# One layer block's gate projection and attention output as seven products with accumulating transfers

## The reference

```python
def gated_rmsnorm(y, z, w):
    g = (y * jax.nn.silu(z)).astype(jnp.float32).reshape(b, l, N_SSM_GROUPS, D_INNER // N_SSM_GROUPS)
    g = g * lax.rsqrt(jnp.mean(g * g, axis=-1, keepdims=True) + RMS_EPS)
    return (g.reshape(b, l, D_INNER) * w.astype(jnp.float32)).astype(y.dtype)

def hybrid_layer(x, w_in, conv_w, conv_b, dt_bias, a_log, d_skip, ssm_norm_w, sinks, w_out, ln_g, ln_b):
    proj = jnp.einsum("bld,de->ble", x, w_in)
    q, k, v, z_attn, z_ssm, xbc, dt_raw = jnp.split(proj, IN_SPLITS, axis=-1)
    attn = sliding_window_attention(q, k, v, sinks) * jax.nn.silu(z_attn)
    xbc = jax.nn.silu(causal_depthwise_conv(xbc, conv_w, conv_b))
    ...
    y = ssd_chunked(xs, dt, a, bm, cm)
    y = y + (xs.reshape(b, l, N_SSM_HEADS, SSM_HEAD_DIM) * d_skip[:, None]).reshape(b, l, D_INNER)
    ssm = gated_rmsnorm(y, z_ssm, ssm_norm_w)
    out = jnp.einsum("ble,ed->bld", jnp.concatenate([attn, ssm], axis=-1), w_out)
    return layer_norm(DEEPNORM_ALPHA * x + out, ln_g, ln_b)
```

## Time and profile before

| | |
|---|---|
| median of 3 runs | 1929.64 us |
| the profiled execution | 1927.62 us |
| its span | 1925.8 us |
| PE busy in the span | 1566.3 us (81%) |
| DVE, ACT busy | 681.8 us (35%), 304.8 us (16%) |
| PE clock in the first 500 us | full (1.00) |

### The profile page before, as it was taken

One profiled execution on the slowest core, in us unless ns is written; L12 is line 12 of the kernel. 1 busy time (PEld: TensorE's weight loads), 2 busy tenths in 40 slices (PEclk: granted clock), 3 DMA queues, 4 the chain that ended last, 5 costly groups with the idle time before them and its releaser, 6 DMA issues.

```text
span 1925.8 us, 20585 instructions
## 1 busy us (share of the span) xinstructions
PE 1566.3 (81%) x8874; PEld 892.2 (46%) x8874; DVE 681.8 (35%) x1395; ACT 304.8 (16%) x804; POOL 13.0 (1%) x39
## 2 busy tenths in 40 slices
PE   9999999999999999766555656655665556799999
PEld 7775567755667845222212222212222122357886
DVE  3663455634486864311111111101111111144533
ACT  1343313432122102000000000000000000213220
POOL 0000000000000000000000000000000000000000
PEclk9999999999999999978778888788887888899999
DMA  9851376414243456999999999999999999954300
GB/s 378 280 151 46 107 275 219 131 53 165 97 171 136 176 218 264 429 430 430 432 431 428 433 428 430 434 428 431 429 429 432 432 431 428 375 197 171 127 10 22
DMA packets 87779, 554.35 MB, mean 288 GB/s; under 512 B 4512, under 2 KB 11424, under 8 KB 74112
## 3 DMA queue, kind: packets, MB, share of 16 engines
q1 hardware_dynamic: 86544, 548.81, 71.0%
q0 software_dynamic: 1136, 4.10, 0.6%
HBM read 551.85 MB, written 1.05 MB: 287 GB/s over the span
## 4 chain that ended last, share of the span: by engine, by line
PE 60%; DMA 35%; DVE 4%; ACT 1%; issue 0%; POOL 0%; SPq 0%; DVEq 0%; ACTq 0%; POOLq 0%
PE bank L679 27%; DMA ring<-in_w 22%; DMA arena<-in_w 12%; PE bank L1174 8%; PE bank L706 7%; PE bank L688 6%; PE bank L1202 3%; PE bank L667 3%; PE bank L1487 1%; PE bank L878 1%; PE bank L811 1%; PE bank L791 1%; DVE arena L2427 0%; PE bank L1145 0%; PE bank L1225 0%
## 5 line engine op out<-in xcount | busy, mean ns | idle before, releaser
L1174 PE MATMUL bank<-ring,arena 128*32 128x512 f32 x1216 | 283.4, 726 | 147.1 <-DMA arena<-in_w 96.7
L1174 PE MATMUL bank<-arena 128*32 128x512 f32 x832 | 228.9, 722 | 101.1 <-DMA ring<-in_w 101.1
L679 PE MATMUL bank<-ring,arena 128*128 128x512 f32 (+3 forms) x744 | 304.5, 560 | 0.8 <-ACT tmp L1543 0.8
L679 PE MATMUL bank<-arena,ring 128*128 128x256 f32 (+1 forms) x1632 | 291.9, 337 | 0.5 <-DVE arena L3106 0.5
L679 PEld LDWEIGHTS bank<-arena,ring 128*128 128x128 f32 x1632 | 256.5, 191 | 30.6 <-issue 7.5
L679 PEld LDWEIGHTS bank<-ring,arena 128*128 128x128 f32 x744 | 138.5, 191 | 129.9 <-issue 118.6
L1174 PEld LDWEIGHTS bank<-ring,arena 128*32 128x32 f32 x1216 | 71.4, 131 | 266.6 <-issue 266.6
L1202 PE MATMUL bank<-ring,arena 128*32 128x512 f32 x576 | 126.4, 681 | 27.8 <-DMA arena<-in_w 18.8
L1174 PEld LDWEIGHTS bank<-arena 128*32 128x32 f32 x832 | 56.3, 130 | 186.2 <-issue 186.0
L706 PE MATMUL bank<-ring,arena 128*128 128x512 f32 (+1 forms) x320 | 127.4, 555 | 1.6 <-DVE arena L2029 0.8
L1202 PE MATMUL bank<-arena 128*32 128x512 f32 x384 | 102.7, 696 | 20.8 <-DMA ring<-in_w 20.8
(11 more groups left out here) (396 smaller groups left out, 1477.1 us busy)
## 6 DMA issues: line engine op xcount, KB each, us to landing
ring<-in_w SPq DMA_DIRECT2D x53, 4096.0 KB, 31.6
arena<-in_w SPq DMA_DIRECT2D x35, 4096.0 KB, 37.7
ring<-in_w_in SPq DMA_DIRECT2D x40, 2048.0 KB, 8.2
ring<-in_w_mod SPq DMA_DIRECT2D x6, 2048.0 KB, 12.5
ring<-in_w_out SPq DMA_DIRECT2D x6, 2048.0 KB, 7.9
arena<-in_w SPq DMA_DIRECT2D x6, 2048.0 KB, 10.5
ring<-in_w SPq DMA_DIRECT2D x6, 2048.0 KB, 12.5
ring<-in_w_out SPq DMA_DIRECT2D x16, 512.0 KB, 9.2
```

The costliest lines, as they stand in the source:

```text
L679: i = te.matmul(ps, lhsT, rhs, start=n0 + k == 0, stop=n0 + k == n - 1)
L1174: m = te.matmul(ps[32 * j:32 * j + 32, :], LM.xg[:, f, 128 * k + 32 * j:128 * k + 32 * j + 32], vs[j][:, 512 * (k % 2):512 * (k % 2) + 512 ...
```

## The change

`zs` and `oa` are each computed as seven products of half size instead of eight, by sums of quarters of the weights and of the activations. A product here is four matmuls of 128 x 512, `times(k, ...)` with k = 1 to 7. The weights come as four quarters (`w_quads`); two ring buffers w0 and w1 and a third, T, take them. The sums of weights are made by transfers that POOL issues with `accum_op=ADD` into the ring: T's first half += quarter 0 (k = 1), T's second half += its first (2), w1's first half += quarter 3 (3), w0's second half += T's second (4). DVE makes four sums of activations (`layer_token_sums`), before `zs` in the conv stage and before `oa` in the state space part. The results of the seven products are combined by DVE and one ACT operation each, through two buffers `part` and `part1`; those of `oa` are added to ALPHA times h at once, so that `os` has banks of its own. The `zs` strand keeps its turns: seven have a product, and the two between the sixth and the seventh are empty. The turns of ACT's tanh and DVE's gate are placed anew. The rotation over four banks starts before `zs`. POOL's transfers of ln_g and ln_b wait for the sixth product of `oa`. The ring starts at buffer 1 instead of 5.

```diff
+            sums = [ar(22848 + 512 * k, 4, 128) for k in range(4)]
+            part, part1 = ar(22336, 512), ar(6144, 512)
...
-            turn, in_turn = [5], list(range(NR))
+            turn, in_turn = [1], list(range(NR))
...
+                def load_quadrants(name, n, at_):
+                    load(name, (lambda v: v.rearrange("p (q c) n -> p q (c n)", q=2),
+                                w_quads[ly, n, at_:at_ + 2].rearrange("q p n -> p q n")))
...
+                load_quadrants(("zs", ly, 0), 0, 0)
+                load_quadrants(("zs", ly, 1), 0, 2)
+                load_quadrants(("T", "zs", ly), 0, 2)
+                load_quadrants(("oa", ly, 0), 1, 0)
+                load_quadrants(("T", "oa", ly), 1, 2)
+                load_quadrants(("oa", ly, 1), 1, 2)
...
+            def layer_seven(name, ly, xT):
+                w0, w1, T = weights((name, ly, 0)), weights((name, ly, 1)), weights(("T", name, ly))
+                lo, hi = slice(0, 128), slice(128, 256)
+                S = L1.sums
+                def times(k, x, w):
+                    ps = fresh("P", name, ly, k, b=4 + ((k - 1) if name == "zs" else k + 6) % 4)
+                    product(ps[:, :], [(x[:, c, :], w[:, c, :]) for c in range(4)]).then_inc(*t.done("mm", "P", name, ly, k))
+                t.wait_ge(*at.of("w", (name, ly, 0)))
+                times(1, xT[:, 0:4, lo], w0[:, 0:4, :])
+                yield
+                times(2, xT[:, 4:8, lo], w0[:, 4:8, :])
+                yield
+                ready(("w", (name, ly, 1)), ("S", name, ly))
+                times(3, S[3], w1[:, 4:8, :])
+                yield
+                ready(("T", name, ly, 1), ("T", name, ly, 2))
+                times(4, S[1], T[:, 4:8, :])
+                yield
+                times(5, S[0], T[:, 0:4, :])
+                yield
+                ready(("T", name, ly, 3))
+                times(6, S[2], w1[:, 0:4, :])
+                t.also("used", (name, ly, 1))
+                yield
+                if name == "zs":
+                    yield
+                    yield
+                ready(("T", name, ly, 4))
+                times(7, xT[:, 4:8, hi], w0[:, 4:8, :])
+                t.also("used", (name, ly, 0))
+                t.also("used", ("T", name, ly))
+                yield
...
-                for g in range(2):
-                    t.wait_ge(*at.of("w", ("zs", ly, g)))
-                    for tt in range(2):
-                        yield from tok512(("zs", ly, tt, g), hT, weights(("zs", ly, g)), tt)
-                        if tt:
-                            t.also("used", ("zs", ly, g))
-                        yield
                 banks.width = 4
+                yield from layer_seven("zs", ly, hT)
                 ready(*[("ev", "pv", ly, n) for n in range(4)])
-                for n in range(2):
-                    t.wait_ge(*at.of("w", ("oa", ly, n)))
-                    for tt in range(2):
-                        ps = fresh("o", ly, tt, n, b=4 + 2 * tt + n)
-                        prs = tok_pairs(L1.zaT, weights(("oa", ly, n)), tt, 0, 512)
-                        product(ps[:, :], prs[:4], 0, 16)
-                        yield
-                        product(ps[:, :], prs[4:], 4, 16).then_inc(*t.step())
-                        if tt:
-                            t.also("used", ("oa", ly, n))
-                        yield
+                yield from layer_seven("oa", ly, L1.zaT)
...
-                        staged(P[4 + 2 * tt + n][:, :], ("sT", ly), L1.ssmT, weights(("os", ly, n)), tt, 0, 512, 8, 16
-                               ).then_inc(*t.done("mm", "o", ly, tt, n))
+                        staged(fresh("o", ly, tt, n, b=4 + 2 * tt + n)[:, :], ("sT", ly), L1.ssmT, weights(("os", ly, n)),
+                               tt, 0, 512).then_inc(*t.done("mm", "o", ly, tt, n))
...
+                def gate_tanh(tt, g):
+                    to = scratch(("zs", ly, tt, g), 512)
+                    ready(("half", "zs", ly, tt, g))
+                    se.activation(to, L1.zs[:, tt, 512 * g:512 * g + 512], ACT.Tanh).then_inc(*a.done("ev", "zs", ly, tt, g))
+                conv_tanh(CONV[-1])
+                yield
+                ready(("mm", "P", "zs", ly, 1), ("S", "zs", ly))
+                se.mul(L1.part, bank("P", "zs", ly, 1)[:, :], 0.5).then_inc(*a.done("ev", "P", "zs", ly, 1))
+                for gate in (None, None, (0, 0), None, None, (0, 1), (1, 1), None, None):
+                    if gate is not None:
+                        gate_tanh(*gate)
+                    yield
+                ready(("mm", "P", "oa", ly, 1), ("ev", "P", "zs", ly, 7))
+                se.copy(L1.part, bank("P", "oa", ly, 1)[:, :]).then_inc(*a.done("ev", "P", "oa", ly, 1))
+                gate_tanh(1, 0)
+                for _ in range(6):
...
+                    if n == 8:
+                        layer_token_sums("zs", ly, hT)
+                    yield
+                conv_gated(CONV[-1])
+                yield from layer_gate_sums(ly)
+                yield from layer_out_sums(ly)
+            def layer_token_sums(name, ly, xT):
+                lo, hi = slice(0, 128), slice(128, 256)
+                s1, s2, s3, s4 = L1.sums
+                behind()
+                if name == "oa":
+                    ready(("mm", "P", "zs", ly, 6))
+                ve.tensor_tensor(s1, xT[:, 0:4, hi], xT[:, 4:8, hi], ALU.subtract).then_inc(*v.step())
+                ve.tensor_tensor(s3, xT[:, 0:4, lo], xT[:, 0:4, hi], ALU.subtract).then_inc(*v.step())
+                behind()
+                ve.tensor_tensor(s2, s1, xT[:, 0:4, lo], ALU.subtract).then_inc(*v.step())
+                behind()
+                ve.tensor_tensor(s4, xT[:, 4:8, lo], s2, ALU.add).then_inc(*v.done("S", name, ly))
+            def layer_gate_sums(ly):
+                X, Y = L1.part, L1.part1
+                def to_part(dst, k, scale, other, op=ALU.add):
+                    ready(("mm", "P", "zs", ly, k))
+                    behind()
+                    return ve.scalar_tensor_tensor(dst, bank("P", "zs", ly, k)[:, :], scale, other, ALU.mult, op)
+                def half(tt, g, k, other, op):
+                    to_part(L1.zs[:, tt, 512 * g:512 * g + 512], k, 0.5, other, op).then_inc(*v.done("ev", "P", "zs", ly, k))
+                    v.also("half", "zs", ly, tt, g)
+                def gate(tt, g):
+                    gated(("zs", ly, tt, g), L1.zs[:, tt, 512 * g:512 * g + 512], 512)
+                yield
+                yield
+                ready(("ev", "P", "zs", ly, 1))
+                half(0, 0, 2, X, ALU.add)
+                yield
+                to_part(X, 4, 0.5, X).then_inc(*v.done("ev", "P", "zs", ly, 4))
+                yield
+                ready(("mm", "sc", ly, 3, 1))
+                to_part(Y, 5, -0.5, X).then_inc(*v.step())
+                half(0, 1, 3, Y, ALU.subtract)
+                gate(0, 0)
+                yield
+                to_part(X, 6, 0.5, X).then_inc(*v.done("ev", "P", "zs", ly, 6))
+                half(1, 1, 5, X, ALU.subtract)
+                yield
+                layer_token_sums("oa", ly, L1.zaT)
+                yield
+                gate(0, 1)
+                yield
+                half(1, 0, 7, X, ALU.add)
+                gate(1, 1)
+                yield
+            def layer_out_sums(ly):
+                X, Y = L1.part, L1.part1
+                def to_part(dst, k, op, flip=False):
+                    ready(("mm", "P", "oa", ly, k))
+                    behind()
+                    ps = bank("P", "oa", ly, k)[:, :]
+                    return ve.tensor_tensor(dst, *((X, ps) if flip else (ps, X)), op)
+                def residual(tt, g, k, other, op):
+                    hv = h[:, tt, 512 * g:512 * g + 512]
+                    behind()
+                    ve.scalar_tensor_tensor(hv, hv, ALPHA, other, ALU.mult, op).then_inc(*v.step())
+                    ready(("mm", "P", "oa", ly, k))
+                    behind()
+                    ve.tensor_tensor(hv, bank("P", "oa", ly, k)[:, :], hv, ALU.add).then_inc(*v.done("ev", "P", "oa", ly, k))
+                yield
+                yield
+                ready(("ev", "P", "oa", ly, 1))
+                residual(0, 0, 2, X, ALU.add)
+                gated(("zs", ly, 1, 0), L1.zs[:, 1, 0:512], 512)
+                yield
+                to_part(X, 4, ALU.add).then_inc(*v.done("ev", "P", "oa", ly, 4))
+                yield
+                to_part(Y, 5, ALU.subtract, flip=True).then_inc(*v.step())
+                residual(0, 1, 3, Y, ALU.subtract)
+                yield
+                to_part(X, 6, ALU.add).then_inc(*v.done("ev", "P", "oa", ly, 6))
+                residual(1, 1, 5, X, ALU.subtract)
+                yield
+                residual(1, 0, 7, X, ALU.add)
+                yield
...
-                ve.scalar_tensor_tensor(hv, hv, ALPHA, P[4 + 2 * tt + n][:, :], ALU.mult, ALU.add
```

(26 more changed lines are left out.)

36 lines of the change are left out of this document (10 added, 26 removed).

## The result

The changed kernel takes 1938.57 us (median of 10 runs, 1932.13 to 1940.97) against 1929.02 us for the kernel before (10 runs, 1926.31 to 1931.71). Over all runs the ratio is 1.0042, with a 95% interval of 1.0031 to 1.0053 (the medians alone give 1.0050). The forecast was 1929.5 us with a range up to 1936, "the same" at 0.49; the time lies outside. The profiled execution took 1938.1 us; its span is 10.6 us longer than before.

A forecast was written before the change was run, and what follows sets the result against it. PE's list was taken to bound block 1 (the first 490 us). End of attention +3.26, place 2 -9.11, place 3 +6.98, layer seam -1.3 sum to -0.17 us, giving 1929.5 us; range 1922 to 1936.

The forecast's parts named there:

- the walk: Stepping through layer 0 with the old trace's timelines of PE, ACT and DVE to place and size new PE waits.
- first rival: Accumulating transfers of weights are late, deciding from 14 us per MB; at 20 us, 2010 us in all; chance 0.07.
- second: Rival: DVE too late in the conv stage and through its longer list; 5 us slower, 1934.5 us; chance 0.22.
- place 3: Last `oa` product of each layer: PE waits 3.49 us for DVE to empty bank 5; +6.98 us over two layers.
- third: Rival: the wait before the last `oa` product is absent or small; 1922.5 us; chance 0.13.
- place 2: State space, half 0: two product groups removed per layer, new wait of 2.85 us before the first `yb`; -9.11 us in all.
- One term of the sum: Seam between layers: the old wait of 1.96 us goes, the first value product comes 0.9 us late; -1.3 us.
- My bound of 14 us: Time per 1 MB accumulating transfer that the `zs` schedule allows; plain ones were put at 11 us at most.

The follow-up runs named there:

- e4_fill: Changed kernel with matmuls of unused results laid into PE's waits, three before the first `yb`, four before the last `oa` product: 1928.28 us, ratio 0.9995.
- e5_tanh: e3_both with ACT's two gate tanh moved out of the stretch before the first `yb`: 1919.09 us, ratio 0.9942 to the kernel before.
- e6_best: e5_tanh with the bank rotation shifted before the transposes of B and at each layer's end: 1917.52 us, ratio 0.9939 to the kernel before.
- e10_long: e5_tanh with eleven idle dependent DVE operations before each layer's last M: 1943.09 us, ratio 1.0061 to the kernel before.
- e9_short: e5_tanh with two idle dependent DVE operations between the two M before the first `yb`: 1921.22 us, ratio 0.9952 to the kernel before.
- e2_sums: Changed kernel with the four activation sums for `oa` moved behind group 0's chain on DVE: 1932.45 us, ratio 1.0015 to the kernel before.
- e3_both: Changed kernel with both edits, that of e1_bank and that of e2_sums: 1923.42 us, ratio 0.9962 to the kernel before.
- e7_gap: Kernel before, without the change, with seven idle dependent DVE operations before each layer's last M: 1940.55 us, ratio 1.0058.
- e1_bank: Changed kernel with the last `oa` product put into bank 6 instead of bank 5: 1927.47 us, ratio 0.9984 to the kernel before.
- e8_plain: Changed kernel with plain transfers in place of the accumulating ones, sums of weights left out: 1938.49 us, ratio 1.0044 to the kernel before.

## Why the prediction was wrong

**What bounds the kernel, and where it waits** was right. PE's list is the time in block 1, each of the new waits stands where the walk put it, to within 0.1 us, and each has the releaser that was named. No transfer was late (first rival), DVE was in time in the conv stage (second), and the wait at place 3 was there in full (third).

**The step that failed** is in the first paragraph and in the terms of places 2 and 3: "what it loses in work is gained, what it waits for anew is lost", each microsecond alike. I noted the full clock of the stretch as a state of the kernel and carried it over to one in which PE stands still four times for some 3 us. The terms were mis-sized, place 2 by 5.06 us (of them 4.70 half clock) and place 3 by 5.40 (4.75); what the remaining 1.0 us are isn't worked out. With e4_fill, in which PE has work in the waits and keeps its clock, the forecast's time comes out: 1928.28 us against 1929.5. The bounds that I gave for the two waits had no room for it, since they were bounds of the wait's length. One term of the sum doesn't follow from its own rows: a wait of 1.96 us replaced by one of 0.9 is 1.06 us, not 1.3; 1.07 was measured.

Why it mattered so much here: the change removes work exactly where PE's work had been the cover, so the saved 13.76 us were turned into waits almost whole. The balance was near zero, and then the sign was decided by what a wait costs beyond its length.

**The size of the effect** at the places of block 1 and at two of block 2, from all profiles: the loss against the same rows at full speed, a case for each layer.

| wait (us) | loss behind it (us) | kernels |
|---|---|---|
| 0.58 | 0 in all 6 | e5_tanh, e6_best, e10_long |
| 0.94 | 0, 0 | e9_short |
| 1.57 (block 2) | 0 in all 12 | all |
| 1.62 | 1.65, 1.68, 0, 1.67 | e2_sums, e3_both |
| 1.96 (the old seam) | 0, 0 | before, e7_gap |
| 1.97 (block 2) | 1.7 in 5, 0 in 7 | all |
| 2.8 | 1.69, 3.01, 1.66, 0, 3.34, 3.12 | after, e1_bank, e8_plain |
| 3.5 | 1.70, 3.05, 2.85, 3.14, 1.77, 3.11, 1.77, 3.43 | after, e2_sums, e8_plain, e7_gap |
| 8.64 | 3.2, 3.7 | e10_long |

The twelve profiles (before, after and ten experiments) have the two waits of block 2 in common, with the same rows around them. Behind that of 1.57 us none lost anything, behind that of 1.97 us five did (before, e1_bank, e3_both, e5_tanh, e7_gap; 6.53 to 6.56 us to the next like row against 4.87). So the length isn't all: from 1.62 to 2.8 us the same wait brings a loss in one case and none in another; at 3.5 us and more all ten lost. It may also be why the changed kernel's runs spread over 8.8 us and those of before over 5.4. What settles a single case stays open. So does the slow row at the kernel's start, behind a wait of 0.60 us for a transfer: e5_tanh has it too (5.79 us behind 0.57), e8_plain a part of it (4.25 behind 0.47), e2_sums and e10_long with 0.57 and 0.58 not at all, and the granted clock there is 1.00 in each. It is the one thing that speaks against reading the table as if nothing ever followed a wait under 1 us.

**What was left lying**: the two waits could be avoided. Place 3 was a bank number, place 2 the turn of four additions and two tanh. With those edits alone the change gains 0.58% (e5_tanh), 10.3 us of the 13.76 that it removes.

## What to carry to other kernels

A new wait on TensorE, in a stretch that so far ran at full clock, is to be priced at its length plus the half clock that can follow. Here that was nothing behind waits of up to 0.94 us, nothing or 1.7 us behind 1.6 to 2.0, nothing or 1.7 to 3.3 behind 2.8, and 1.7 to 3.4 behind 3.5; look in the trace of before for a wait of that length and at the length of the rows behind it. When work is taken away from the engine that bounds the kernel, first ask what that work was hiding, and move what is asked of the other engines (the turn of an addition, a bank that is still to be read) before the cover goes. Where a wait can't be avoided, matmuls of no use in it can cost less than idling: here they brought back 9 to 10 us.

## What the runs showed of the hardware

The loss behind a wait didn't grow with it beyond 3.5 us: 8.64 us of idle time cost 3.2 and 3.7 us behind them, 3.5 us up to 3.4. Accumulating transfers of 1 MB took 1.6 times (from the weights in HBM into the ring) and 2.1 times (within the ring) as long as plain ones. Issued by POOL, median us from issue to landing, in the changed kernel:

```profile
ring<-in_w_quads POOLq DMA_DIRECT2D x8, 1024.0 KB, 10.9
ring<-ring POOLq DMA_DIRECT2D x8, 1024.0 KB, 9.9
```

And the same transfers without the addition, in e8_plain:

```profile
ring<-in_w_quads POOLq DMA_DIRECT2D x8, 1024.0 KB, 6.7
ring<-ring POOLq DMA_DIRECT2D x8, 1024.0 KB, 4.8
```

My bound of 14 us, from which they would have been late, had room for both.
